# A hybrid two-layer network: the first four maxima turned and placed together, and the activated quarters of the MLP kept by group

## The reference, cut to what matters

```python
h = layer_norm(x, ln_emb_g, ln_emb_b)                    # 1024 tokens x 1024
for l in range(2):
    parts = split_columns(h @ w_in[l])
    y_a = mamba2_ssd(...); y_b = mla(...); y_c = retention(...); y_d = nsa(...)
    mix = jnp.concatenate([y_a, y_b, y_c, y_d], axis=-1) @ w_out[l]
    h = layer_norm(DEEPNORM_ALPHA * h + mix, ln1_g[l], ln1_b[l])
    ff = jnp.square(jax.nn.relu(h @ w_mlp1[l])) @ w_mlp2[l]      # 1024 -> 4096 -> 1024
    h = layer_norm(DEEPNORM_ALPHA * h + ff, ln2_g[l], ln2_b[l])
# inside mla, for each of 4 heads, causal, in tiles of 128 queries:
    s = where(kpos <= qpos, q @ k.T, NEG_INF);  o = softmax(s) @ v
```

## Time and profile before

| | us |
|---|---|
| median of 3 runs | 2842.62 |
| lowest, highest | 2842.02, 2843.44 |
| the profiled execution's own time | 2847.2 |
| its span, first to last instruction | 2845.4 |
| PE busy, mean granted clock | 2720.9, 0.977 |
| DVE busy | 1790.9 |
| ACT busy | 1136.3 |

### The profile page before, as it was taken

How to read it: one execution, slowest core, us unless ns; L and a number is a source line. 1 busy time by engine, 2 the same in 40 slices (tenths; PEclk the granted TensorE clock), 3 DMA queues, 4 the chain that set the end, 5 groups by cost and what they waited for, 6 DMA issues and landing times. The chain is left out here.

```text
span 2845.4 us, 37143 instructions
## 1 busy us (share of the span) xinstructions
PE 2720.9 (96%) x13986; PEld 2183.4 (77%) x13986; DVE 1790.9 (63%) x2939; ACT 1136.3 (40%) x1817; POOL 252.0 (9%) x220
## 2 busy tenths in 40 slices
PE   5999989999989999999999999899999899999997
PEld 5899866656868887888888998566568688878886
DVE  5654554454787776776856444535547877758778
ACT  3322223334355554433433222234343555543343
POOL 3121222000000000000011112220000000000000
PEclk9999989999999999999999999799999999999998
DMA  4223234102315445997621233421032354479875
GB/s 164 71 68 94 91 92 92 31 1 82 103 64 176 143 144 192 384 312 247 225 86 38 77 100 97 101 54 30 1 119 89 97 163 145 141 261 364 290 230 188
DMA packets 254360, 387.29 MB, mean 136 GB/s; under 512 B 38608, under 2 KB 126800, under 8 KB 254184
## 3 DMA queue, kind: packets, MB, share of 16 engines
q1 hardware_dynamic: 254184, 384.92, 42.3%
HBM read 288.05 MB, written 96.83 MB: 135 GB/s over the span
## 5 line engine op out<-in xcount | busy, mean ns | idle before, releaser
L2747 ACT ACTIVATE att_PT<-att_ST 128x512 f32<-128x512 f32 (+2 forms) x244 | 135.3, 554 | 327.3 <-PE att_ST L2639 196.0
L1626 PE MATMUL mix_acc<-mix_whi,x_hi 128*128 128x256 f32 (+1 forms) x640 | 185.5, 290 | 0.0
L998 PE MATMUL dense_tr<-mlp_w,mlp_a 128*128 128x512 f32 x448 | 175.9, 393 | 6.3 <-DVE mlp_w L1302 6.3
L1628 PE MATMUL mix_acc<-mix_whi,x_lo 128*128 128x256 f32 (+1 forms) x640 | 180.1, 281 | 0.0
L1627 PE MATMUL mix_acc<-mix_wlo,x_hi 128*128 128x256 f32 (+1 forms) x640 | 180.0, 281 | 0.0
L1000 PE MATMUL dense_tr<-mlp_w,mlp_a 128*128 128x512 f32 x448 | 174.9, 390 | 0.0
L999 PE MATMUL dense_tr<-mlp_w,mlp_a 128*128 128x512 f32 x448 | 174.9, 390 | 0.0
L998 PE MATMUL dense_acc<-mlp_w,mlp_a 128*128 128x512 f32 x448 | 174.4, 389 | 0.0
L999 PE MATMUL dense_acc<-mlp_w,mlp_a 128*128 128x512 f32 x448 | 174.4, 389 | 0.0
L1000 PE MATMUL dense_acc<-mlp_w,mlp_a 128*128 128x512 f32 x448 | 174.4, 389 | 0.0
L644 POOL TENSOR_TENSOR norm_rstd<-norm_var,norm_power 128x1 f32<-128x1 f32 x32 | 29.8, 932 | 1474.1 <-DVE norm_var L624 1474.1
(11 more groups left out here) (432 smaller groups left out, 7461.1 us busy)
## 6 DMA issues: line engine op xcount, KB each, us to landing
mlp_w_raw<-w_mlp SPq DMA_DIRECT2D x124, 512.0 KB, 6.1
blocks<-h SPq DMA_DIRECT2D x32, 1792.0 KB, 8.4
mlp_a_raw<-blocks SPq DMA_DIRECT2D x72, 512.0 KB, 4.5
mlp_raw<-w_mlp SPq DMA_DIRECT2D x66, 512.0 KB, 6.1
ahead<-w_in SPq DMA_DIRECT2D x20, 1024.0 KB, 6.6
mlp_temp<-blocks SPq DMA_DIRECT2D x38, 512.0 KB, 4.9
residual<-h SPq DMA_DIRECT2D x32, 512.0 KB, 3.9
h<-residual SPq DMA_DIRECT2D x32, 512.0 KB, 9.7
```

The source lines that it names most:

```text
L998: pe.matmul(out, ah, wh, start=(ch == 0 and k == 0), stop=False, skip_group_check=True)
L1626: pe.matmul(out, xh, whi[b][:, k, 0:n], start=(k == 0), stop=False)
L1628: mm = pe.matmul(out, xl, whi[b][:, k, 0:n], start=False, stop=(k == KT - 1))
L2747: act.activation(PT[0:width, n % 3, c0:512], ST[0:width, n % 2, c0:512], ACT.Exp).then_inc(s.exp_ready, 1)
```

## The change

Three places are touched. The first unit of the mixers takes the two passes with high weights of a pair of k as soon as ACT has made that quarter, and the pass with low weights one pair later. In attention, the first four tiles are turned side by side into `maxT`, behind all their maxima, and one DVE instruction places all of them. In the MLP the activated quarters 12 and 21 of a group lie in places 6 and 5 of its own stage; `activate` of groups 0 and 1 waits for no other group, that of later groups for the store of group g-2; ACT's activations and DVE's rests and quarters of group 1 move to position 13, and `block_sums(0)` to position 14, behind them. `block_sums` takes its five sums in another order and waits for the two that read the places that the last two overwrite.

```diff
-        a12, a21 = flat[:, 14 * 512:15 * 512], flat[:, 15 * 512:16 * 512]
+        a12_of, a21_of = (lambda g: stage[g % 2][:, 6, :]), (lambda g: stage[g % 2][:, 5, :])
@@ activate(g, i), ACT
                     act.wait_ge(s.multiplied, at[g, i] + 1)
-                    if g:
-                        act.wait_ge(s.blocks_ready, g)
+                    if g >= 2:
+                        act.wait_ge(blocks_stored[g % 2], 16 * (g // 2))
                     else:
+                        act.wait_ge(s.z_turned, NT)
                         act.wait_ge(s.sum_ready, sum_at[7, HT - 1] + 1)
@@ ACT's loop over the positions
                         elif i == 2:
                             if g == 2:
-                                activate(1, 4)
-                                activate(1, 3)
                                 square(1, 6)
                             square(g - 1, 7)
...
                     elif (g, i) == (1, 7):
                         square(0, 7)
+                        activate(1, 4)
+                        activate(1, 3)
@@ block_sums(g), DVE
-                    for i in (1, 2, 5, 6, 7):
+                    for n, i in enumerate((2, 5, 1, 6, 7)):
                         (a, b), op = PRODUCTS[i].left
+                        if i in (6, 7):
+                            dve.wait_ge(s.quarter_read, 2 * g + n - 2)
                         mm = dve.tensor_tensor(stage[g % 2][:, i - 1, :], part[a], part[b], op)
+                        if i in (2, 5):
+                            mm.then_inc(s.quarter_read, 1)
                     mm.then_inc(s.blocks_ready, 1)
@@ collect(p), DVE
                         elif (g, i) == (2, 2):
-                            rests(1)
-                            quarter22(1)
-                            quarter11(1)
-                    elif (g, i) == (0, 1):
-                        rests(0)
-                    elif (g, i) == (1, 7):
-                        block_sums(0)
+                            block_sums(0)
+                    elif (g, i) in ((0, 1), (1, 7)):
+                        gather(g)
+                        rest12(g)
+                        rest21(g)
+                        rest1(g)
+                        if g:
+                            quarter22(g)
                     if i == 6 and g != 1:
                         quarter22(g)
-                    elif i == 7 and g != 1:
+                    elif i == 7:
                         quarter11(g)
@@ features_unit, PE
+                    if unit == 0:
+                        for part in range(5):
+                            if part < 4:
+                                pe.wait_ge(s.first_hi, part + 1)
+                                for k in (2 * part, 2 * part + 1):
+                                    pe.matmul(out, whi[b][:, k, cols], hi[:, k, half * 512:(half + 1) * 512], start=(k == 0), stop=False)
+                                    pe.matmul(out, whi[b][:, k, cols], lo[:, k, half * 512:(half + 1) * 512], start=False, stop=False)
+                            if part:
+                                pe.wait_ge(s.first_lo, part)
+                                for k in (2 * part - 2, 2 * part - 1):
+                                    mm = pe.matmul(out, wlo[b][:, k, cols], hi[:, k, half * 512:(half + 1) * 512], start=False, stop=(k == KT - 1))
+                        mm.then_inc(s.unit_done, 1)
+                        return
                     for k in range(KT):
-                        if unit == 0 and k % 2 == 0:
-                            pe.wait_ge(s.first_lo, k // 2 + 1)
@@ attention, PE, ahead of the loop of steps
                     for u_ in first_units:
                         maxima([(u_, at) for at in range(len(pieces[u_]))])
-                        if u_:
-                            turn_maxima(u_ - 1)
-                    turn_maxima(first_units[-1])
+                    for u_ in first_units:
+                        pe.wait_ge(s.max_ready, u_ + 1)
+                        pe.transpose(maxT[0:H, tile_at(u_)], negm[:, u_, 0:H], ident[:]).then_inc(s.m_turned, 1)
@@ attention, DVE, ahead of the loop of steps
                         maxima([(u_, at) for at in range(len(pieces[u_]))])
-                        if u_ >= 2:
-                            place(u_ - 2)
-                    for u_ in first_units[-2:]:
-                        place(u_)
+                    first_cols = len(first_units) * P
+                    dve.wait_ge(s.m_turned, len(first_units))
+                    by_tile = [H, H, len(first_units), P]
+                    dve.tensor_tensor(q2[QD:QD + H, :, 0:first_cols].rearrange("p h (u q) -> p h u q", q=P),
+                                      maxT[0:H, 0:first_cols].rearrange("p (u q) -> p u q", q=P).unsqueeze(1).to_broadcast(by_tile),
+                                      pick[0:H].unsqueeze(2).to_broadcast(by_tile), ALU.mult).then_inc(s.m_placed, len(first_units))
```

More of the change, by code:

```diff
@@ L1074, in activate @@
                 def activate(g, i):
-                    dst, bank, relu, ready = (a12, tr[:, g % 2, :], s.relu12, s.ready12) if i == 4 else (a21, acc[:, g % 2, :], s.relu21, s.ready21)
+                    dst, bank, relu, ready = (a12_of(g), tr[:, g % 2, :], s.relu12, s.ready12) if i == 4 else (a21_of(g), acc[:, g % 2, :], s.relu21, s.ready21)
                     act.wait_ge(s.multiplied, at[g, i] + 1)
-                    if g:
-                        act.wait_ge(s.blocks_ready, g)
+                    if g >= 2:
+                        act.wait_ge(blocks_stored[g % 2], 16 * (g // 2))
                     else:
+                        act.wait_ge(s.z_turned, NT)
                         act.wait_ge(s.sum_ready, sum_at[7, HT - 1] + 1)
@@ L1231, in block_sums @@
                 def block_sums(g):
-                    part = {(0, 0): stage[g % 2][:, 2, :], (1, 1): stage[g % 2][:, 3, :], (0, 1): a12, (1, 0): a21}
+                    part = {(0, 0): stage[g % 2][:, 2, :], (1, 1): stage[g % 2][:, 3, :], (0, 1): a12_of(g), (1, 0): a21_of(g)}
                     dve.wait_ge(s.ready22, 2 * g + 2)
```

## The result

| | before | after |
|---|---|---|
| median, us (10 runs each, side by side) | 2842.31 | 2850.01 |
| lowest, highest | 2840.18, 2843.82 | 2846.50, 2852.46 |
| span of the profiled execution | 2845.4 | 2848.4 |

The ratio is 1.003, 95% interval 1.0021 to 1.0039: 7.7 us slower by the medians (8.5 by the ratio), 1.1 us from the 2848.9 of the forecast and inside its range. The two spans differ by only 3.0 us, because the profiled execution of the kernel before lies 4.6 us above its median, at a mean clock of 0.977, and that of the changed kernel (2850.19 us, 0.979) at its median. So the traces are compared stage by stage and not by their spans.

What follows compares the result with a forecast made beforehand. TensorE, busy 96% of the span, was taken as the bound. Terms -1.5 - 4.3 + 10.1 + 2.0 = +6.3 us took the profiled 2847.2 to 2853.5, carried over to 2848.9 us; range 2838 to 2854.5.

Steps and rivals of the forecast that it cites:

- part one: Mixers' first unit: PE needs only ACT's first quarter and starts 0.73 us earlier a layer, -1.5 us in all.
- part two: Attention's first maxima: one placement of 2.32 us, tail 2.9 us, scores 2.15 us earlier a layer, -4.3 in all.
- (2,3): PE product in the MLP's opening, waiting for ACT's copy5: claimed to start about 3.9 us earlier.
- DVE's left sum behind the load: MLP's opening: DVE's sum after group 3's weights land, claimed to begin at 863.5 instead of 857.87.
- (2,6): PE product in the MLP's opening needing a low made by DVE: claimed 1.3 us later, after an 8 us wait.
- (2,7): PE product in the MLP's opening waiting for ACT's copy1: claimed at 871.45 against 866.37, +5.1 us a layer.
- clock, a layer: Lower PE clock from (2,7) on, after idle gaps in the MLP's opening: taken +1.0 us, bounds 0 to 3.4.
- sum: All terms over both layers: -1.5 - 4.3 + 10.1 + 2.0 = +6.3 us.
- The mechanism: MLP's opening: group 0's later sums hold its store and group 3's load on SP's queue 5.65 us longer.
- part three: Quarters of the MLP: copy5's wait shrinks, but group 3's load goes out later; +10.1 us in all.
- The landing: Group 3's weights in the MLP: taken to land 10.5 us after issue, bounds 5.5 to 11.1.
- The carrying over: Profiled execution forecast at 2853.5 us, lowered to 2848.9 because the profiled one before lay 4.6 us above the median.

Runs made afterwards that it cites:

- e2: Kernel before with part three alone, the activated quarters of the MLP in places by group: 2854.06 us, ratio 1.0037.
- e4: Changed kernel with one edit in SP's list, the load of group 3's weights ahead of the store of group 0's blocks: 2836.95 us, ratio 0.9984.
- e12: Changed kernel; SP still waits for group 0's sums, then issues the load of group 3's weights ahead of group 0's store: 2845.63 us, ratio 1.0004.
- e5: e4 with the even groups' activated quarters back in the two places the kernel before had for them: 2824.07 us, ratio 0.9938.
- e11: Kernel before with one added wait, holding the load of group 3's weights until DVE has done group 1's last quarter: 2845.70 us, ratio 1.0006.
- e3: Kernel before with the load of group 3's weights issued ahead of the store of group 0's blocks: 2840.55 us, ratio 0.9997.
- e7: Kernel before with part two alone, the first four tiles' maxima turned side by side and placed at once: 2842.13 us, ratio 0.9996.
- e8: Kernel before with part one alone, the mixers' first products not waiting for the low weights: 2840.12 us, ratio 0.9993.
- e10: e5 with two ACT instructions moved: copy2 of group 2 ahead of position 19's split, copy5 ahead of group 1's squares: 2827.18 us, ratio 0.9945.
- e9: Changed kernel, its load still late, with the even groups' activated quarters in two places of their own: 2850.50 us, ratio 1.0026.

## Why the prediction was right, and where it was not

| step | forecast | measured |
|---|---|---|
| part one, a layer | -0.73 | -0.73 in the trace (ACT's first quarter to PE's start) |
| part two, placement / tail | 2.32 / 2.9 us | 2.29 / 2.88 us |
| part two, a layer | -2.15 | -2.0 in the mean of the traces |
| (2,3) | 3.9 earlier | 3.9 earlier |
| DVE's left sum behind the load, in the times of the kernel before | 863.5 | 863.4 |
| (2,6) | 1.3 later | 1.2 and 2.5 later |
| (2,7) | 5.1 later | 4.9 and 4.9 later |
| clock, a layer | +1.0 | +1.9 |
| sum | +6.3 | +7.7 by the medians, +8.5 (6.0 to 11.1) by the ratio |

**The mechanism** was the one of the forecast: each row it named as its proof is there, e2 has the whole loss with part three alone, and e4 takes the 7.7 us wait away with one edit in SP's list. The rule of the Trainium skill that was weighed (DMA: Bandwidth & Descriptors, "Issuing engines are not separate DMA queues") prices only the issue itself. Read as the whole cost of sharing SP's list it would have kept part three's gain; e2 measured part three 10.5 us slower. The rule isn't refuted by this: the 5.6 us lie ahead of the issue, at the head of SP's list behind a semaphore, of which that section says nothing. To them comes the landing, 10.4 us where the load needs 6.2 or 6.3 when it isn't right behind the store.

**The landing** was right for a reason that I had only half: I took 10.5 us "because store and load still start 0.4 us apart". The start 0.4 us apart is not enough: in e12 it is the same and the load lands in 6.3 us. The order of the two decides which of them takes 10.5 us.

**The clock** was undersized. From (2,7) to the first chunk of the second product it took 252.2 and 252.3 us before, 254.4 and 253.9 after: +1.9 a layer, of which one stretch of 3.4 us at half clock is 1.7. (In the first layer 0.6 is a longer wait for the chunk.) I had bounded this by 0 to 3.4 and taken 1.0. The 1.8 us that this term lacked over both layers are of the size of the 1.4 us (medians) to 2.2 us (ratio) by which the sum fell short. For the mixers' start the forecast assumed half clock; the changed kernel's first layer ran it at full clock, which the 28 layer starts above do not put down to part one.

**The carrying over** was right. The forecast for a profiled execution was 2853.5, and it took 2850.2. The 4.6 us that were taken off went with that one execution of the kernel before, at a clock of 0.977. The measured terms of the table add up to +8.1 us, between the +7.7 of the medians and the +8.5 of the ratio. That the forecast came within 1.1 us of the median says little by itself: the interval of the measurement is 2.5 us to either side, and the forecast's part two and part three were each off by 0.3, in opposite directions. Some of its sums are rounded by up to 0.1 us; nothing rests on it.

**Left unsaid** was the second wait. The prediction had the activation's wait for the store, and found it hidden behind the load. That was right for this change, but it hides only as long as the load is late: e4 and e5 put its price at 13 us. And I read DVE's 5.73 us idle in the kernel before as a load that bounds. For (2,7) it was near bounding, as e11 has it 0.8 us later with the landing 0.8 us later. But with that wait taken away e3 is only 0.9 us faster (3.4 faster to 2.0 slower), since PE was on its low clock there in the first layer.

Not settled: what e7 and e8 gain alone, which the runs can't tell from nothing; whether part one spares a stretch of low clock; whether the load would land sooner if it left from another engine's list than the store's, which no run tried; and whether the order of ACT's activations, or DVE's sums of group 1 placed later, would close the last gaps of e5 and e10.

## What to carry to other kernels

A move on one engine is also a move of every transfer that waits for its result, and of every transfer queued behind that one: before an engine's work is postponed, list what stands behind it on SP's queue, and issue the load that is already free ahead of the store that is not. After a gap is closed, look for the waits that ended just before it; two side by side cost no more than the later of them. Taking away the one that ends first gains nothing (e9), the one that ends last gains part (e4), and only both give the whole (e5). An engine's long wait is no bound as long as the engine that uses its result is itself not ready sooner.

## What the runs showed of the hardware

- **Of two transfers that leave 0.4 us apart on SP's queue, the second takes most of the delay.** The load lands in 6.3 us with the store behind it (e12) and in 10.4 behind the store (the changed kernel); 5.4 us behind the store it takes 6.2 (e11). The store takes 6.8 with the load that far behind (e11), 8.4 with the load right behind it (the changed kernel) and 10.5 behind the load (e12). The second layers agree within 0.6 us. All of them left from SP's list; no run shows two lists.
- **Idle gaps of 1.9 to 2.8 us may or may not cost the clock.** In the mixers' start of the first layer PE was idle 2.03 us and the window behind it has PEclk 1.00 (above). In e7 it was idle 2.76 us at that place and the window 64.83 to 68.21 has 1.00 too (the row below), while the kernel before has 0.51 after the same 2.76. Before the MLP's opening PE was idle 1.85 us and the clock fell.
- **The time of one execution goes with its mean granted clock.** In 93 runs of the kernel before the mean time is 2845.6 us at a clock of 0.977 (12 runs), 2843.3 at 0.979 (25) and 2840.6 at 0.981 (13): about 1.3 us for each 0.001. This is under half of the scatter (0.44 of its variance, with a clock known to 0.001); the times spread from 2833.9 to 2848.6, which is why effects of 2 us needed the traces.

```profile
64.83:68.21 3.38, 3.38 (x15) 2.80 (x16) 1.75 (x3) 0.78 (x2) 0.00 (x0) 1.00 0.63 5
```
